# First up projection of a two-block transformer kernel: one 512-column matmul for both parts of the activation

## Chip, cores and metric

The kernel runs on 1 core of one Trainium2 chip. The metric is the device time of one execution in microseconds (us). TensorE, VectorE, ScalarE, GpSimd and SyncE are called PE, DVE, ACT, POOL and SP, as in the profile; PEld is the load of a stationary operand into TensorE.

## What is computed

Two transformer blocks are computed one after the other on 256 tokens of width 2048, in float32. The change lies in the feed-forward part of the first block, and there in the product with `w_up`:

```python
D_FF = 11 * D_MODEL // 4          # 5632

def conv_ffn(h, w_up, w_conv, b_conv, w_down):      # h: (1, 256, 2048)
    z = h @ w_up                                    # (1, 256, 11264)
    z1 = jnp.pad(z[:, :-1], ((0, 0), (1, 0), (0, 0)))
    z2 = jnp.pad(z[:, :-2], ((0, 0), (2, 0), (0, 0)))
    z = w_conv[0] * z2 + w_conv[1] * z1 + w_conv[2] * z + b_conv
    gate, val = jnp.split(z, 2, axis=-1)
    return (jax.nn.gelu(gate) * val) @ w_down

def first_block(x, c, ...):
    ...                                             # modulation vectors, token mixing
    h = rms_norm(x, g_pre_ffn[l]) * (1.0 + sc2) + sh2
    y = conv_ffn(h, w_up[l], w_conv[l], b_conv[l], w_down[l])
    x = x + gt2 * rms_norm(y, g_post_ffn[l])
```

The second block has attention, a state-space scan and a feed-forward part of its own (silu instead of the convolution). It is not changed.

## The kernel before

Each large product is made with two parts of each operand in a rounded format (`float32r`): a high part `hi` and the remainder `lo = x - hi`. A product is then the sum of three matmuls, hi x lo, lo x hi and hi x hi (the helper `three`, lines 2097 to 2101).

**The weights.** All weights stream from HBM as 484 groups of 1 MB, [128, 4, 512] each. SP loads a group into one of four slots (`raw`, line 339) as soon as TensorE has counted the group that used the slot four groups earlier (`pe_used`). ACT makes its high part `w_hi` (line 819), DVE its low part `w_lo` (line 1312), which is written over the raw slot. TensorE waits for `lo_made` at the head of each group (`begin_group`). All engines run an order that is written out by hand; nothing moves on its own.

**The first up projection** (in the profile about 720 to 1225 us) has 22 chunks of 512 weight columns. A chunk is 4 groups; a group is 4 contraction tiles x 4 column tiles x 3 matmuls. Here the weights are the stationary operand and the activation (`h2T_hi`, `h2T_lo`, 256 tokens wide) is the moving one, so each matmul has 256 columns (`cols_chunk`). The result [128, 4, 256] of a chunk fills one of two buffers of two PSUM banks each (`acc0`, `acc1`); the banks `tp0`, `tp1`, `ms0`, `ms1` serve transposes and small things.

**After a chunk** ACT and DVE run `up1(c)`, in this order, with `split()` for the making of a weight part:

| step | ACT | DVE |
|---|---|---|
| 1 | last tap and bias, from PSUM, 4 instructions (L1043) | waits for it (`z_mid`) |
| 2 | `w_hi` of the next chunk's third group | the two other taps, from PSUM, 8 instructions (L1664) |
| 3 | waits for `z_conv`, then gelu (L1050) | `w_lo` of the next chunk's third group |
| 4 | `w_hi` of its fourth group | gate times value (L1672), `w_lo` of the fourth group |
| 5 | high part of the hidden activation (L1054) | its low part (L1678) |
| 6 | `w_hi` of the first two groups of the chunk after that | their `w_lo` |
| 7 | | for the first 16 chunks: `ada_group`, 4 chained instructions on 1 MB of the modulation weights (L1366, L1368) |

So when TensorE ends a chunk, two groups of the next one are ready, and the third becomes ready by steps 1 to 3. The loads of the slots for step 6 are released when TensorE ends the first and the second group of the chunk that it is in. After chunk 21 the down projection starts, in chunks with 512 moving columns; the third group of it is made after `up1(21)`.

**At the entry** (`even_out`) the second chunk holds additional TensorE work whose result nobody reads: 12 matmuls of 512 columns, 8 transposes and the two matmuls of `settle`.

## Time and profile before

| | before |
|---|---|
| median of 3 runs | 3042.03 us (3038.48 to 3045.42) |
| profiled execution: time, span | 3043.16 us, 3041.4 us |
| granted TensorE clock, mean over the span | 0.982 |
| busy: PE, PEld, DVE, ACT, POOL | 96%, 84%, 61%, 42%, 11% |
| chain that ended last: PE, DVE, DMA, ACT | 87%, 6%, 2%, 2% |

A row of the trace gives the start, the length, the engine, the source line, the operation and its operands; brackets at its end hold the time in which the engine was idle before it, and what ended that. Matmuls overlap in the trace: the cost of one in a stream is the distance from its start to the next start, and not its own length. The same holds, to a smaller degree, for instructions on DVE and ACT. The result tile of the up projection, `zc`, has the name `bias_rows` in the profile, since it lies in that buffer.

### The profile page before, as it was taken

Reading aid. Unit: us, or ns where it says so; the run is one execution under the profiler, and the core shown is the slowest. Engines: PE = TensorE matmul, PEld = TensorE weight load, DVE = VectorE, ACT = ScalarE, POOL = GpSimd, SP = SyncE. Lnnn points to the kernel's source line nnn. Section 1 sums busy time; section 2 is a strip of 40 time slices with the busy share of each in tenths; the row PEclk is TensorE's granted clock in tenths of the full one; section 3 lists DMA queues with packets and bytes.
Section 4 is the critical chain, followed back from the end, with each engine's and each line's share of the span. In section 5 each row is a group of like instructions: output and inputs, shape, how many; then the busy total and the mean of one; then the engine's idle time right before and its main releaser. Section 6 shows DMA issues by size and latency. Waiting matters only on the chain.

```text
span 3041.4 us, 42782 instructions
## 1 busy us (share of the span) xinstructions
PE 2932.4 (96%) x17832; PEld 2560.8 (84%) x17832; DVE 1866.7 (61%) x1884; ACT 1268.0 (42%) x1228; POOL 326.9 (11%) x467
## 2 busy tenths in 40 slices
PE   7999999997999999999799999989999999999998
PEld 3687777877999999888687878867889999999886
DVE  5877777796677776554545456755555555555444
ACT  2334544335444444343524333443444434343333
POOL 1000000000000000000104946610000000000000
PEclk9999999998999999999899998989999999999999
DMA  9877877894566655575546652226645555555554
GB/s 408 354 276 277 298 270 293 292 372 175 222 230 239 227 200 183 202 256 207 193 158 215 220 170 77 92 79 221 244 180 184 193 192 194 192 192 207 207 219 166
DMA packets 109903, 667.32 MB, mean 219 GB/s; under 512 B 23504, under 2 KB 25744, under 8 KB 33360
## 3 DMA queue, kind: packets, MB, share of 16 engines
q1 hardware_dynamic: 101584, 626.96, 56.1%
q0 software_dynamic: 8208, 38.80, 3.5%
q8 instruction: 79, 1.29, 0.2%
q14 instruction: 32, 0.26, 0.0%
HBM read 646.24 MB, written 19.48 MB: 219 GB/s over the span
## 4 chain that ended last, share of the span: by engine, by line
PE 87%; DVE 6%; DMA 2%; ACT 2%; SPq 1%; issue 1%; POOL 0%; DVEq 0%; ACTq 0%; POOLq 0%
PE acc L2099 27%; PE acc L2101 27%; PE acc L2100 27%; DVE w_lo L1312 2%; DMA ada<-ada_stream 2%; PE tp L2148 1%; DVE mod_sum L1368 1%; PE ms L2172 1%; ACT w_hi L819 1%; DMA w_raw<-w_stream 1%; PE acc L2645 0%; SPq L440 0%; PE ms L2099 0%; PE ms L2100 0%; PE ms L2101 0%
## 5 line engine op out<-in xcount | busy, mean ns | idle before, releaser
L1312 DVE TENSOR_TENSOR w_lo<-w_raw,w_hi 128x2048 fp32r<-128x2048 f32 (+1 forms) x484 | 1103.9, 2289 | 742.7 <-ACT w_hi L819 723.7
L819 ACT ACTIVATE w_hi<-w_raw 128x2048 fp32r<-128x2048 f32 (+1 forms) x484 | 918.9, 1907 | 895.6 <-DMA w_raw<-w_stream 893.4
L2099 PE MATMUL acc<-h2T_hi,w_lo 128*128 128x256 f32 x2816 | 786.0, 279 | 0.0
L2100 PE MATMUL acc<-h2T_lo,w_hi 128*128 128x256 f32 x2816 | 785.2, 279 | 0.0
L2101 PE MATMUL acc<-h2T_hi,w_hi 128*128 128x256 f32 x2816 | 785.2, 279 | 0.0
L2101 PEld LDWEIGHTS acc<-h2T_hi,w_hi 128*128 128x128 f32 x2816 | 535.4, 190 | 0.0
L2099 PEld LDWEIGHTS acc<-h2T_hi,w_lo 128*128 128x128 f32 x2816 | 529.8, 188 | 0.1
L2100 PEld LDWEIGHTS acc<-h2T_lo,w_hi 128*128 128x128 f32 x2816 | 529.8, 188 | 0.1
L2099 PE MATMUL acc<-w_hi,hid_lo 128*128 128x512 f32 x704 | 274.6, 390 | 0.9 <-DVE w_lo L1312 0.9
L2101 PE MATMUL acc<-w_hi,hid_hi 128*128 128x512 f32 x704 | 274.0, 389 | 0.0
L2100 PE MATMUL acc<-w_lo,hid_hi 128*128 128x512 f32 x704 | 273.9, 389 | 0.0
L2099 PE MATMUL acc<-w_hi,h1T_lo 128*128 128x512 f32 x576 | 232.9, 404 | 10.1 <-DVE w_lo L1312 10.1
L1368 DVE SCALAR_TENSOR_TENSOR mod_sum<-ada,cond,mod_sum 128x512 f32<-128x512 f32 x300 | 225.3, 751 | 24.6 <-DMA ada<-ada_stream 15.5
L2100 PE MATMUL acc<-w_lo,h1T_hi 128*128 128x512 f32 x576 | 226.1, 393 | 0.0
L2101 PE MATMUL acc<-w_hi,h1T_hi 128*128 128x512 f32 x576 | 226.0, 392 | 0.0
L2099 PEld LDWEIGHTS acc<-w_hi,hid_lo 128*128 128x128 f32 x704 | 132.2, 188 | 28.6 <-DVE w_lo L1312 1.3
L2101 PEld LDWEIGHTS acc<-w_hi,hid_hi 128*128 128x128 f32 x704 | 132.2, 188 | 27.7
L2100 PEld LDWEIGHTS acc<-w_lo,hid_hi 128*128 128x128 f32 x704 | 132.2, 188 | 27.1
L2099 PEld LDWEIGHTS acc<-w_hi,h1T_lo 128*128 128x128 f32 x576 | 109.1, 189 | 39.4 <-issue 15.2
L2099 PE MATMUL acc<-w_hi,nT_lo 128*128 128x512 f32 x320 | 126.6, 396 | 5.2 <-DVE w_lo L1312 5.2
L2101 PEld LDWEIGHTS acc<-w_hi,h1T_hi 128*128 128x128 f32 x576 | 109.1, 189 | 23.6
L2100 PEld LDWEIGHTS acc<-w_lo,h1T_hi 128*128 128x128 f32 x576 | 109.3, 190 | 21.8 <-issue 0.5
(530 smaller groups left out, 3869.1 us busy)
## 6 DMA issues: line engine op xcount, KB each, us to landing
w_raw<-w_stream SPq DMA_DIRECT2D x484, 1024.0 KB, 4.8
ada<-ada_stream SPq DMA_DIRECT2D x80, 1024.0 KB, 7.0
ada_first<-ada_stream SPq DMA_DIRECT2D x16, 1024.0 KB, 12.0
g_dram<-gates_out SPq DMA_DIRECT2D x12, 512.0 KB, 7.4
gates_in<-g_dram POOLq DMA_DIRECT2D x12, 512.0 KB, 6.0
bias_rows<-b_in POOLq DMA_DIRECT2D x18, 256.0 KB, 6.7
x_res<-x POOLq DMA_DIRECT2D x2, 2048.0 KB, 12.5
x_dram<-x_res POOLq DMA_DIRECT2D x2, 2048.0 KB, 7.9
```

The lines of the kernel that those rows point to most:

```text
L819: sc.activation(whi[:, s % 4, :, 0:w], raw[:, s % 4, :, 0:w], ACT.Copy).then_inc(hi_made, 1)
L1312: v.tensor_tensor(wlo[:, s % 4, :, 0:w], raw[:, s % 4, :, 0:w], whi[:, s % 4, :, 0:w].bitcast(F32), ALU.subtract).then_inc(lo_made, 1)
L1368: chain(v.scalar_tensor_tensor(macc[:], slots[b][:, q], cond[:, k:k + 1], macc[:], ALU.mult, ALU.add))
L2099: mm(o, sl, mh, start=start, stop=False, skip_group_check=share)
L2100: mm(o, sh, ml, start=False, stop=False, skip_group_check=share)
L2101: return mm(o, sh, mh, start=False, stop=stop, skip_group_check=share)
L2148: ins = tr(t[0:w, c:c + n], src, ident[0:n, 0:n])
L2172: ins = mm(ms[c % 2][:], cond[:, k:k + 1].to_broadcast([P, P]), adaf[n % 4][:, q], start=k == 0, stop=k == KD - 1)
```

## The change

The two matmuls with `w_hi` as the stationary operand become one with 512 moving columns: the high part of the activation and the low part side by side (`h2Tb`). The bank of a column tile then holds two halves of 256 columns whose sum is the result. A chunk takes four whole banks, the four of `acc` and those of `tp` and `ms` in turn (`wide_banks`). DVE adds the halves of each bank into a new SBUF tile `zs` with a reduction and hands it to ACT (`z_sum`); the taps read `zs` instead of PSUM. The banks are given free after this addition. `even_out` and `settle` are gone, a wait is added ahead of the first wide chunk and one ahead of the fourth group of the down projection.

```diff
+        zs = u("z_sum", [P, 4, S], X0 + 8)
...
-        h2T = [u("h2T_hi", [P, KD, S], -B64, F32R), u("h2T_lo", [P, KD, S], 16 - B64, F32R)]
+        h2Tb = u("h2T", [P, 2, KD, S], -B64, F32R)
+        h2T = [h2Tb[:, 0], h2Tb[:, 1]]
...
+        def wide_banks(n):
+            return [t[:] for t in tp + ms] if n % 2 else [acc[i][:, j] for i in range(2) for j in range(2)]
...
 # ScalarE
             def up1(c, last=False):
-                act.wait_ge(pe_used, upc.n * 4 + (G_IN1 + G_MERGE + G_OUT1 + 4))
+                act.wait_ge(sem("z_sum"), upc.n + 1)
...
-                    ins = sc.activation(zc[:, f], bank(upc.slot)[:].rearrange("p a (b s) -> p (a b) s", s=S)[:, f],
+                    ins = sc.activation(zc[:, f], zs[:, f],
...
 # VectorE
             def up1(c, last=False):
-                b = bank(chunks.slot)[:].rearrange("p a (b s) -> p (a b) s", s=S)
+                dve.wait_ge(pe_used, upc.n * 4 + (G_IN1 + G_MERGE + G_OUT1 + 4))
+                for f, b in enumerate(wide_banks(chunks.slot)):
+                    ins = v.reduce_sum(zs[:, f], b.rearrange("p (a s) -> p s a", s=S), AX.X)
+                chain(ins)
+                dve.sem_inc(acc_free, 1)
+                dve.sem_inc(sem("z_sum"), 1)
                 chunks.add()
                 dve.wait_ge(sem("z_mid"), upc.n + 1)
...
-                        ins = v.scalar_tensor_tensor(zc[:, f, sh:S], b[:, f, 0:S - sh], wv, zc[:, f, sh:S],
+                        ins = v.scalar_tensor_tensor(zc[:, f, sh:S], zs[:, f, 0:S - sh], wv, zc[:, f, sh:S],
...
-                dve.sem_inc(acc_free, 1)
                 dve.sem_inc(sem("z_conv"), 1)
...
 # TensorE
-            cols_chunk(h2T, quarters(y1, 0))
-            cols_chunk(h2T, even_out)
-            up_pairs(FC // 2 - 1)
+            def wide_chunk(ahead=None):
+                banks = wide_banks(chunks.slot)
+                chunks.add()
+                for g in range(KD // GK):
+                    if ahead:
+                        ahead(g)
+                    s = begin_group()
+                    for f in range(4):
+                        for q in range(GK):
+                            k = g * GK + q
+                            mm(banks[f][:, 0:S], wlo[:, s, q, f * P:(f + 1) * P], h2T[0][:, k],
+                               start=k == 0, stop=False, skip_group_check=True)
+                            ins = mm(banks[f].rearrange("p (a s) -> p a s", s=S), whi[:, s, q, f * P:(f + 1) * P], h2Tb[:, :, k],
+                                     start=False, stop=k == KD - 1, skip_group_check=True)
+                    end_group(ins)
+
+            pe.wait_ge(acc_free, chunks.n)
+            wide_chunk(quarters(y1, 0))
+            turned()
+            wide_chunk()
+            with engine_loop(pe, FC // 2 - 1, (m, 8), (chunks, 2)) as i:
+                for _ in range(2):
+                    pe.wait_ge(acc_free, chunks.n - 1)
+                    wide_chunk()
...
             def gate2(i):
+                if i == 3:
+                    pe.wait_ge(acc_free, chunks.n - 1)
```

The up projection of the second block keeps the three matmuls of 256 columns.

TensorE, before, the end of the first chunk and the start of the second. The first three rows are one product of a weight tile; the next three are from `even_out`, with `ms` as their output.

```order
L2099 MATMUL acc<-h2T_hi,w_lo 128x256
L2100 MATMUL acc<-h2T_lo,w_hi 128x256
L2101 MATMUL acc<-h2T_hi,w_hi 128x256
L2099 MATMUL ms<-w_hi,w_lo 128x512
L2100 MATMUL ms<-w_lo,w_hi 128x512
L2101 MATMUL ms<-w_hi 128x512
```

TensorE, after, at the same place (`h2T` is now both parts in one tensor; the second chunk writes `tp` and `ms`).

```order
L2457 MATMUL acc<-h2T,w_lo 128x256
L2459 MATMUL acc<-h2T,w_hi 128x512
L2457 MATMUL acc<-h2T,w_lo 128x256
L2459 MATMUL acc<-h2T,w_hi 128x512
L2457 MATMUL tp<-h2T,w_lo 128x256
L2459 MATMUL tp<-h2T,w_hi 128x512
```

Two instructions stand where there were three, the columns are the same 768, and the run at the entry is gone.

DVE, before, from the last `w_lo` of the first chunk's `up1` to the gelu product of the second.

```order
L1312 TENSOR_TENSOR w_lo<-w_raw,w_hi 128x2048 [waits hi_made] x2
L1366 TENSOR_SCALAR mod_sum_0_79<-ada_0_77,cond 128x512 [waits ada_in0]
L1368 SCALAR_TENSOR_TENSOR mod_sum_0_79<-ada_0_77,cond,mod_sum_0_79 128x512 [waits dve_chain] x3
L1664 SCALAR_TENSOR_TENSOR bias_rows<-acc,conv_taps,bias_rows 128x255 [waits dve_chain,z_mid]
L1664 SCALAR_TENSOR_TENSOR bias_rows<-acc,conv_taps,bias_rows 128x255 x3
L1664 SCALAR_TENSOR_TENSOR bias_rows<-acc,conv_taps,bias_rows 128x254 [waits dve_chain]
L1664 SCALAR_TENSOR_TENSOR bias_rows<-acc,conv_taps,bias_rows 128x254 x3
L1312 TENSOR_TENSOR w_lo<-w_raw,w_hi 128x2048 [waits dve_chain,hi_made]
L1672 TENSOR_TENSOR bias_rows<-bias_rows 128x512 [waits z_gelu]
```

DVE, after, the same stretch.

```order
L1317 TENSOR_TENSOR w_lo<-w_raw,w_hi 128x2048 [waits hi_made] x2
L1371 TENSOR_SCALAR mod_sum_0_79<-ada_0_77,cond 128x512 [waits ada_in0]
L1373 SCALAR_TENSOR_TENSOR mod_sum_0_79<-ada_0_77,cond,mod_sum_0_79 128x512 [waits dve_chain] x3
L1664 TENSOR_REDUCE z_sum<-tp 128x256 [waits dve_chain,pe_used]
L1664 TENSOR_REDUCE z_sum<-tp 128x256
L1664 TENSOR_REDUCE z_sum<-ms 128x256 x2
L1674 SCALAR_TENSOR_TENSOR bias_rows<-z_sum,conv_taps,bias_rows 128x255 [waits dve_chain,z_mid]
L1674 SCALAR_TENSOR_TENSOR bias_rows<-z_sum,conv_taps,bias_rows 128x255 x3
L1674 SCALAR_TENSOR_TENSOR bias_rows<-z_sum,conv_taps,bias_rows 128x254 [waits dve_chain]
L1674 SCALAR_TENSOR_TENSOR bias_rows<-z_sum,conv_taps,bias_rows 128x254 x3
L1317 TENSOR_TENSOR w_lo<-w_raw,w_hi 128x2048 [waits dve_chain,hi_made]
L1681 TENSOR_TENSOR bias_rows<-bias_rows 128x512 [waits z_gelu]
```

Four reductions stand between the modulation sums and the taps. The step that released ACT before, the end of TensorE's chunk, now releases DVE, and ACT starts after the reductions.

## Rows read from the trace of the kernel before

**Rows 1.** The page: chain that ended last by line, and a costly group

```profile
PE acc L2099 27%; PE acc L2101 27%; PE acc L2100 27%; DVE w_lo L1312 2%; DMA ada<-ada_stream 2%; PE tp L2148 1%; DVE mod_sum L1368 1%; PE ms L2172 1%; ACT w_hi L819 1%; DMA w_raw<-w_stream 1%; PE acc L2645 0%; SPq L440 0%; PE ms L2099 0%; PE ms L2100 0%; PE ms L2101 0%
...
L2099 PE MATMUL acc<-h2T_hi,w_lo 128*128 128x256 f32 x2816 | 786.0, 279 | 0.0
```

**Rows 2.** Busy time by stretch: us, PE, PEld, DVE, ACT, POOL, clock, DMA, GB/s

```profile
900.00:1000.00 100.00, 100.00 (x851) 100.00 (x850) 72.23 (x78) 44.87 (x42) 0.00 (x0) 1.00 0.62 228
```

**Rows 3.** Timeline of PE in the down projection (start, length)

```profile
1300.06 0.39 PE L2099 MATMUL acc<-w_hi,hid_lo 128*128 128x512 f32 x1
...
1302.78 0.39 PE L2099 MATMUL acc<-w_hi,hid_lo 128*128 128x512 f32 x1
```

**Rows 4.** Timeline of DVE, one chunk of the up projection

```profile
956.36 3.34 DVE L1664 SCALAR_TENSOR_TENSOR bias_rows<-acc,conv_taps,bias_rows 128x255 f32<-128x255 f32 x8 [1.55 <-ACT bias_rows L1043]
959.95 2.29 DVE L1312 TENSOR_TENSOR w_lo<-w_raw,w_hi 128x2048 fp32r<-128x2048 f32 x1 [0.24 <-DVE bias_rows L1664]
962.15 0.68 DVE L1672 TENSOR_TENSOR bias_rows<-bias_rows 128x512 f32<-128x512 f32 x1
962.99 2.29 DVE L1312 TENSOR_TENSOR w_lo<-w_raw,w_hi 128x2048 fp32r<-128x2048 f32 x1
965.20 0.69 DVE L1678 TENSOR_TENSOR hid_lo<-bias_rows,hid_hi 128x512 fp32r<-128x512 f32 x1
966.72 2.29 DVE L1312 TENSOR_TENSOR w_lo<-w_raw,w_hi 128x2048 fp32r<-128x2048 f32 x1 [0.84 <-ACT w_hi L819]
972.37 2.29 DVE L1312 TENSOR_TENSOR w_lo<-w_raw,w_hi 128x2048 fp32r<-128x2048 f32 x1 [3.37 <-ACT w_hi L819]
974.58 3.11 DVE L1368 SCALAR_TENSOR_TENSOR mod_sum<-ada,cond,mod_sum 128x512 f32<-128x512 f32 x4
978.97 3.34 DVE L1664 SCALAR_TENSOR_TENSOR bias_rows<-acc,conv_taps,bias_rows 128x255 f32<-128x255 f32 x8 [1.28 <-ACT bias_rows L1043]
982.56 2.29 DVE L1312 TENSOR_TENSOR w_lo<-w_raw,w_hi 128x2048 fp32r<-128x2048 f32 x1 [0.25 <-DVE bias_rows L1664]
```

**Rows 5.** Timeline of ACT, the same chunk

```profile
954.39 1.93 ACT L1043 ACTIVATE bias_rows<-acc,conv_taps 128x256 f32<-128x256 f32 x4 [4.67 <-PE acc L2101]
...
970.43 1.92 ACT L819 ACTIVATE w_hi<-w_raw 128x2048 fp32r<-128x2048 f32 x1 [3.74 <-DMA w_raw<-w_stream]
977.01 1.93 ACT L1043 ACTIVATE bias_rows<-acc,conv_taps 128x256 f32<-128x256 f32 x4 [4.66 <-PE acc L2101]
```

**Rows 6.** Timeline of SP's DMA queue, issue of the second slot's load

```profile
965.63 0.33 SPq L339 DMA_DIRECT2D w_raw<-w_stream  x1
```

**Rows 7.** Nearest rows for the reductions and for reading SBUF on ACT

```profile
L1445 DVE TENSOR_REDUCE mod_part<-tp 128x4 f32<-128x512 f32 x16 | 11.0, 685 | 4.6 <-PE tp L2148 4.5
...
699.83 0.58 ACT L968 ACTIVATE bias_rows<-acc 128x512 f32<-128x512 f32 x1
...
704.28 0.63 ACT L968 ACTIVATE bias_rows<-x_res 128x512 f32<-128x512 f32 x1 [3.06 <-DVE x_res L1592]
```

**Rows 8.** Timeline of ACT, DVE and PE where the down projection begins

```profile
1225.54 1.94 ACT L1043 ACTIVATE bias_rows<-acc,conv_taps 128x256 f32<-128x256 f32 x4 [4.40 <-PE acc L2101]
...
1234.96 2.29 DVE L1312 TENSOR_TENSOR w_lo<-w_raw,w_hi 128x2048 fp32r<-128x2048 f32 x1 [1.12 <-ACT w_hi L819]
...
1237.31 0.50 PE L2099 MATMUL acc<-w_hi,hid_lo 128*128 128x512 f32 x1 [0.93 <-DVE w_lo L1312]
```

**Rows 9.** Timeline of ACT, starts of the first two `up1`

```profile
746.61 1.93 ACT L1043 ACTIVATE bias_rows<-acc,conv_taps 128x256 f32<-128x256 f32 x4 [5.07 <-PE acc L2101]
...
773.28 1.93 ACT L1043 ACTIVATE bias_rows<-acc,conv_taps 128x256 f32<-128x256 f32 x4 [4.33 <-PE acc L2101]
```

**Rows 10.** Timeline of PE after two waits, and the stretches that follow them

```profile
394.28 0.48 PE L2148 MATMUL tp<-ident,scores 128*128 128x128 f32 x1 [3.44 <-DVE scores L1540]
...
1652.66 0.50 PE L2099 MATMUL acc<-w_hi,nT_lo 128*128 128x512 f32 x1 [2.79 <-DVE w_lo L1312]
...
394.00:400.80 6.80, 6.52 (x15) 4.58 (x16) 5.20 (x9) 4.39 (x6) 0.00 (x0) 0.50 0.40 167
...
1653.50:1657.00 3.50, 3.50 (x10) 2.74 (x9) 1.49 (x1) 3.29 (x3) 3.04 (x7) 0.51 0.56 234
```

More of the change, by code:

```diff
@@ L2406, in _ @@
                     mod_turn(macc2[n - 1])
-            def settle():
-                for t in range(TT):
-                    mm(ms[1][:, t * P:(t + 1) * P], ones[:].to_broadcast([P, P]), ident[:], start=True, stop=True)
             def quarter(src, n):
@@ L2441, in up_pairs @@
                         cols_chunk(h2T)
-            def even_out(g):
-                if g == 0:
-                    s = m.slot % 4
-                    pe.wait_ge(lo_made, m.n + 1)
-                    for q in range(GK):
-                        three(ms[0][:], whi[:, s, q, 0:P], wlo[:, s, q, 0:P], whi[:, s, q], wlo[:, s, q], q == 0, q == GK - 1)
-                if g == 2:
-                    for q in range(8):
-                        tr(ms[1][:, q % 4 * P:(q % 4 + 1) * P], ident[:], ident[:])
-                if g == 3:
-                    settle()
-            cols_chunk(h2T, quarters(y1, 0))
-            cols_chunk(h2T, even_out)
-            up_pairs(FC // 2 - 1)
+            def wide_chunk(ahead=None):
[21 more added lines that the diff above has]
+                    wide_chunk()
             def gate2(i):
+                if i == 3:
+                    pe.wait_ge(acc_free, chunks.n - 1)
                 if 3 <= i <= 6:
```

## The prediction, written before the changed kernel ran

> **What bounds the kernel now.** I read the chain that ended last first. By line, the three matmul lines of the helper `three` hold 27% each of the span [rows 1]; the reader is to see that TensorE sets the time nearly everywhere. The group of the up projections has 0.0 us of idle time before its 2816 instructions [rows 1]. Then I read busy time by stretch inside the first up projection: in 100 us TensorE starts 851 matmuls at a granted clock of 1.00, and DVE is busy for 72 us of them [rows 2]. So TensorE is the bound, but DVE has only 28 us of 100 to spare, and the timelines of DVE, ACT and the DMA queue decide what happens when TensorE gets faster and DVE gets more to do.
>
> The mean length of a matmul (279 ns [rows 1]) is no price. 100 us by 851 starts is 117.5 ns for one with 256 columns [rows 2]. A chunk ends where ACT's first step starts: from 954.39 to 977.01 is 22.62 us [rows 5], by 192 matmuls 117.8 ns. With 512 columns, 12 matmuls lie between 1300.06 and 1302.78 [rows 3]: 226.7 ns.
>
> **Term 1, the matmuls.** Before, a tile costs 3 x 117.8 = 353.4 ns, after 117.8 + 226.7 = 344.5 ns. The columns are the same 768; only one fixed cost of 8.9 ns goes. It doesn't save a third. A chunk has 64 tiles: 0.57 us less, 22.05 us. All 22 chunks: 12.5 us if TensorE never waits.
>
> **Term 2, what DVE and ACT get.** Four reductions of 512 elements each. The nearest row is a reduction that reads 512 elements of PSUM in 685 ns [rows 7], with fewer outputs (4, not 256). Instructions of one kind start a little before the last one's end (a `w_lo` of 2.29 us is followed after 2.21 [rows 4]), so I take 0.61 us each and 2.52 us for four. From the end of a chained instruction over its semaphores to the next is 0.25 us after the taps [rows 4] and 0.16 after the gelu product (962.15 + 0.68 to 962.99 [rows 4]); I take 0.20 from the reductions to ACT. ACT then reads SBUF, not PSUM: 0.63 against 0.58 us for 512 elements [rows 7], 0.2 us for its four. The taps on DVE I leave unchanged.
>
> What hides this? From ACT's first step to the end of the third group's `w_lo` passed 982.56 + 2.29 - 977.01 = 7.84 us [rows 4, 5]. It becomes 2.52 + 0.20 + 7.84 + 0.2 = 10.76, plus 0.06 until TensorE starts (1237.25 to 1237.31 [rows 8]): 10.82. TensorE has two ready groups, 22.05 / 2 = 11.02 us. In a chunk before which DVE is idle it just fits, with 0.2 us to spare, and costs nothing.
>
> In the 16 chunks that follow an `ada_group` DVE isn't idle. It ends the modulation sums at 974.58 + 3.11 = 977.69 [rows 4], 0.68 us after TensorE's chunk. That cost nothing, since ACT came first; now the reductions queue behind it. This makes a closed loop through the ring of slots. TensorE ends the second group and releases its slot's load at 965.63 [rows 6]; ACT's `w_hi` follows at 970.43 [rows 5], then `w_lo`, then the sums to 977.69: 12.06 us. Then 0.16 until the first reduction, 2.52 + 0.20, then 8.04, then 0.06: 23.04 us from the end of a chunk's second group to the start of the next chunk's third. If TensorE waits s there, a chunk takes P = 22.05 + s and the loop spans P + s. So s = (23.04 - 22.05) / 2 = 0.50 us and P = 22.55: against 22.62 only 0.07 us is gained in each. DVE's own work in that period, in series, is 2.52 + 0.20 + 5.75 (ACT's step and the taps) + 2.20 + 0.84 + 2.21 + 0.75 + 2 x 2.21 + 3.11 + 0.16 = 22.16 us [rows 4, 5]. It fits, with 0.4 us to spare, so the load's loop is the tighter one.
>
> The stage: 16 x 0.07 + 6 x 0.57 = 4.5 us gained of the 12.5.
>
> **Term 3, the start of the down projection.** After the last chunk two groups of the down projection are ready. Already TensorE waits 0.93 us for the third [rows 8]. The chain from 1225.54 to the `w_lo` at 1234.96 depends on ACT and DVE alone [rows 8], and it grows by 2.52 + 0.20 + 0.2 = 2.9 us: the wait becomes 3.85, 2.9 us lost, and no work of TensorE's takes its place.
>
> The wait has a second price. A TensorE wait of 3.44 us was followed by a stretch at half clock (1.2 GHz) to 400.8, and one of 2.79 us by 3.5 us at 0.51 [rows 10]. At half clock matmuls take double, so these cost (400.8 - 394.3) / 2 = 3.3 and about 1.7 us. For a wait of 3.85 us I take the middle, 2.5.
>
> **Term 4, the entry run.** The second chunk took 773.28 - 746.61 = 26.67 us [rows 9], 4.05 more than 22.62. This is wholly on TensorE's path, and it goes. The added waits for free banks cost nothing: DVE frees a bank 3 us after a chunk's end, a whole chunk before it is written again, and the transposes' banks are copied before their turn. Two modulation loads start in the same place and come nearer to the next weight loads; up to 1 us, not in the sum.
>
> **The sum**, against the profiled execution's span of 3041.4 us and time of 3043.16: -4.5 + 2.9 + 2.5 - 4.05 = -3.15, giving a time of 3040.0. The median shown is 1.1 us lower, so I forecast 3038.9 us, 0.1% less. I call a difference of under 0.2% (6 us) no difference that this kernel's runs can tell.
>
> **Rivals.**
>
> *The waits don't come, faster.* All 12.5 us arrive if the loop is a microsecond shorter than I make it (by slightly shorter loads or a reduction that costs less), and the clock holds. -12.5 - 4.05 + 2.9 = -13.7: 3028.4 us. For it: the margin is half a microsecond in a loop of 23. Against it: every link of the loop is a row of one chunk, and the reductions can't be much under 512 elements' time. Halfway cases land near 3034.
>
> *The reductions cost by outputs too, slower.* No row shows a reduction with 256 outputs. If each output took a slot beside the inputs, 768 elements: the slope between 512 and 2048 elements, (2.29 - 0.69) / 1536 = 1.04 ns [rows 4], gives 0.95 us each, 3.58 for four, 1.06 more. DVE's series becomes 23.22 and is then the bound of the 16 chunks: +0.60 each, 9.6 us. In the other six the third group comes at 11.88 instead of 11.02, +0.29 each, 1.7. With 2.9 + 1.1 + 2.5 at the down projection and -4.05 this is +13.8: 3055.8 us. It decides against the change from about 0.85 us per reduction. The bounds of the price are these: 0.61 and 0.95; I take the low end, since the row read the same number of elements from the same memory.
>
> *The pair of matmuls costs what three did.* If cost goes with columns (the two parts lie 16 KB apart and no row reads such an operand), 512 columns cost 2 x 117.8 and the chunk stays at 22.62 us. The loop then gives (23.04 + 22.62) / 2 = 22.83 in the 16 chunks, +3.4 us; nothing in the six; +5.4 and -4.05: +4.7, 3046.7 us. For it: the fixed cost of 8.9 ns comes from two stages with different neighbours. Against it: both are long streams at full clock.
>
> The Trainium skill ("TensorE: Matmul & The Clock Gate", Back-to-back issue gap) gives a warm gap of N/2.4 + 2.5 ns. By it the dropped fixed cost is 2.5 ns, 0.16 us a chunk and 3.5 us in all instead of 12.5, which lies between this rival and my Term 1. The rows here show larger gaps, 117.8 against its 109.2 and 226.7 against its 215.8; I go by the rows.
>
> **How the numbers follow.** Forecast 0.50 (3034 to 3044: 0.2 us in the loop is 1.6 us, the clock after the wait 0 to 3.4), faster rival 0.17, slower 0.13, no cheaper pair 0.12, something not seen 0.08. The range 3030 to 3052 leaves out the far ends of the first two rivals. Faster by over 0.2%: 0.17, plus 0.08 from the forecast's lower edge and 0.02 unseen, 0.27. Slower: 0.13 plus 0.02 and 0.04, 0.19. Within: 0.54.
>
> **What the profile after would show.** Starts of TensorE's pairs 344 ns apart. Chunks of about 22.55 us in the first 17 and 22.05 in the last five, with a wait of about 0.5 us on `w_lo` at the third group in 16 of them. Four reductions with a length of 0.69 us, 2.5 together, the first starting when the modulation sums end. A TensorE wait near 3.9 us at the down projection's third group and half clock behind it. The second chunk without its 4 us. I am wrong if the pair is dearer, the reductions take above 0.8 us, or no third group waits.

## The result

| | before | after |
|---|---|---|
| median | 3041.42 us (3025.1 to 3045.42, 12 executions) | 3049.81 us (3047.87 to 3055.81, 12 executions) |
| ratio after / before | | 1.0036, 95% interval 1.0025 to 1.0048 |
| profiled execution: time, span | 3043.16, 3041.4 us | 3050.85, 3049.1 us |
| granted TensorE clock, mean | 0.982 | 0.982 |

The kernel became slower by 8.4 us, 0.28% by the medians and 0.36% by the paired ratio. I had forecast 3038.9 us. The time lies in my range of 3030 to 3052, but a slowdown of over 0.2% was the side to which I gave 0.19.

The page of the changed kernel: the chain that ended last by line, then the two groups of instructions that took over the stage (busy us, mean ns | idle before).

```profile
PE acc L2108 21%; PE acc L2109 21%; PE acc L2110 21%; PE acc L2459 3%; DVE w_lo L1317 3%; DVE mod_sum L1373 2%; DMA w_raw<-w_stream 2%; PE acc L2457 2%; PE ms L2459 2%; PE tp L2459 2%; DMA ada<-ada_stream 2%; PE tp L2157 1%; ACT w_hi L824 1%; PE ms L2181 1%; DVE bias_rows L1674 1%
...
L2459 PE MATMUL acc<-h2T,w_hi 128*128 128x512 f32 x704 | 251.4, 400 | 0.0
...
L2457 PE MATMUL acc<-h2T,w_lo 128*128 128x256 f32 x704 | 199.7, 284 | 1.8 <-DVE w_lo L1317 1.6
```

The three matmul lines have less of the chain than in [rows 1], since L2457 and L2459 took over the stage, and the making of `w_lo`, the modulation sums, the loads and the taps now stand in it. The stage itself, in the columns of [rows 2]:

```profile
900.00:1000.00 100.00, 98.90 (x557) 85.19 (x556) 82.88 (x94) 45.47 (x42) 0.00 (x0) 1.00 0.62 227
```

TensorE is no longer busy all the time, and DVE has 17 us of 100 to spare, not 28. How dear is a pair? Its timeline in an unbroken stretch:

```profile
959.78 0.28 PE L2457 MATMUL acc<-h2T,w_lo 128*128 128x256 f32 x1
959.90 0.40 PE L2459 MATMUL acc<-h2T,w_hi 128*128 128x512 f32 x1
...
960.84 0.28 PE L2457 MATMUL acc<-h2T,w_lo 128*128 128x256 f32 x1
```

Between the two starts of L2457 lie three pairs: 1.06 us / 3 = 353 ns. The three matmuls of before took 3 x 117.8 = 353.4 ns (22.62 us by 192, [rows 5]). The pair costs the same. I had 344.5.

The same chunk boundary as in [rows 4 to 6], after: SP's queue, ACT, DVE, and then TensorE's first matmul of the third group.

```profile
966.83 0.33 SPq L344 DMA_DIRECT2D w_raw<-w_stream  x1
...
989.44 0.33 SPq L344 DMA_DIRECT2D w_raw<-w_stream  x1
...
995.98 0.33 SPq L344 DMA_DIRECT2D w_raw<-w_stream  x1
```

```profile
971.55 1.92 ACT L824 ACTIVATE w_hi<-w_raw 128x2048 fp32r<-128x2048 f32 x1 [2.12 <-DMA w_raw<-w_stream]
981.91 2.08 ACT L1048 ACTIVATE bias_rows<-z_sum,conv_taps 128x256 f32<-128x256 f32 x4 [8.44 <-DVEq L1667]
```

```profile
973.50 2.29 DVE L1317 TENSOR_TENSOR w_lo<-w_raw,w_hi 128x2048 fp32r<-128x2048 f32 x1 [1.47 <-ACT w_hi L824]
975.71 3.11 DVE L1373 SCALAR_TENSOR_TENSOR mod_sum<-ada,cond,mod_sum 128x512 f32<-128x512 f32 x4
978.97 2.48 DVE L1664 TENSOR_REDUCE z_sum<-acc 128x256 f32<-128x512 f32 x4
984.02 3.37 DVE L1674 SCALAR_TENSOR_TENSOR bias_rows<-z_sum,conv_taps,bias_rows 128x255 f32<-128x255 f32 x8 [2.58 <-ACT bias_rows L1048]
987.54 2.29 DVE L1317 TENSOR_TENSOR w_lo<-w_raw,w_hi 128x2048 fp32r<-128x2048 f32 x1
```

```profile
989.89 0.39 PE L2457 MATMUL tp<-h2T,w_lo 128*128 128x256 f32 x1 [0.62 <-DVE w_lo L1317]
...
1245.30 0.79 PE L2108 MATMUL acc<-w_hi,hid_lo 128*128 128x512 f32 x1 [3.65 <-DVE w_lo L1317]
...
1662.47 0.50 PE L2108 MATMUL acc<-w_hi,nT_lo 128*128 128x512 f32 x1 [1.68 <-DVE w_lo L1317]
```

Read it as a chain. The load issued at 966.83 reaches DVE's `w_lo` at 973.50; the modulation sums follow, then the reductions, which start 0.15 us after the sums end. ACT starts at 981.91, and TensorE gets its third group at 989.89 after 0.62 us of idleness. So the closed loop of the forecast is there, with its parts in the order given. The second TensorE row is the boundary to the down projection, where the 0.93 us of [rows 8] became 3.65. Behind it the clock fell:

```profile
1245.30:1251.20 5.90, 5.90 (x14) 4.64 (x15) 5.90 (x3) 3.12 (x2) 0.00 (x0) 0.50 0.11 43
```

**The account** (chunks are counted from 0). From ACT's first step of chunk 0 to that of chunk 21 (21 chunks) it is 1233.46 - 750.45 = 483.0 us. Before it was 1225.54 - 746.61 = 478.9 [rows 8, 9], of which 4.05 were the entry run. So 21 chunks cost 8.1 us more. Chunk 0 itself ends 1.1 us later: TensorE's next matmul starts at 747.51 against 746.41. Of this, 0.56 us was there when chunk 0 started (720.89 against 720.33). The four rows, before and then after:

```profile
720.33 0.56 PE L2099 MATMUL acc<-h2T_hi,w_lo 128*128 128x256 f32 x1
...
746.41 0.39 PE L2099 MATMUL ms<-w_hi,w_lo 128*128 128x512 f32 x1
```

```profile
720.89 0.56 PE L2457 MATMUL acc<-h2T,w_lo 128*128 128x256 f32 x1
...
747.51 0.28 PE L2457 MATMUL tp<-h2T,w_lo 128*128 128x256 f32 x1
```

With -4.05 this is +5.2 us where the down projection starts. The longer wait adds 3.65 - 0.93 = 2.7, the half clock 5.9 / 2 = about 2.95: +10.9. Some 3 us come back at a later place: before, a wait of 2.79 us was followed by 3.5 us at half clock [rows 10]; after, the same wait is 1.68 (the third TensorE row) and no half clock follows, 1.1 + 1.7 us. The sum, +8.0, stands against +7.7 between the spans.

### The profile page after: what moved, and what is told of

Read it like the earlier page. It is cut to its first block, busy times and chain, and to the rows that moved or that the text cites. A ratio compares the mean times of both kernels' runs of the same rounds, so it can differ in the third digit from the quotient of the medians.

```text
span 3049.1 us, 40010 instructions
## 1 busy us (share of the span) xinstructions
PE 2932.6 (96%) x16400; PEld 2492.3 (82%) x16400; DVE 1919.2 (63%) x1972; ACT 1269.5 (42%) x1228; POOL 332.1 (11%) x467
## 4 chain that ended last, share of the span: by engine, by line
PE 81%; DVE 9%; DMA 4%; ACT 3%; issue 1%; SPq 1%; POOL 0%; ACTq 0%; DVEq 0%; POOLq 0%
PE acc L2108 21%; PE acc L2109 21%; PE acc L2110 21%; PE acc L2459 3%; DVE w_lo L1317 3%; DVE mod_sum L1373 2%; DMA w_raw<-w_stream 2%; PE acc L2457 2%; PE ms L2459 2%; PE tp L2459 2%; DMA ada<-ada_stream 2%; PE tp L2157 1%; ACT w_hi L824 1%; PE ms L2181 1%; DVE bias_rows L1674 1%
## 5 line engine op out<-in xcount | busy, mean ns | idle before, releaser
L2108 PE MATMUL acc<-h2T,w_lo 128*128 128x256 f32 x1408 | 389.0, 276 | 0.0
L2109 PE MATMUL acc<-h2T,w_hi 128*128 128x256 f32 x1408 | 388.9, 276 | 0.0
L2110 PE MATMUL acc<-h2T,w_hi 128*128 128x256 f32 x1408 | 388.8, 276 | 0.0
L2110 PEld LDWEIGHTS acc<-h2T,w_hi 128*128 128x128 f32 x1408 | 264.4, 188 | 0.0
L2109 PEld LDWEIGHTS acc<-h2T,w_hi 128*128 128x128 f32 x1408 | 264.3, 188 | 0.0
L2108 PEld LDWEIGHTS acc<-h2T,w_lo 128*128 128x128 f32 x1408 | 264.3, 188 | 0.0
L2459 PE MATMUL acc<-h2T,w_hi 128*128 128x512 f32 x704 | 251.4, 400 | 0.0
L2457 PE MATMUL acc<-h2T,w_lo 128*128 128x256 f32 x704 | 199.7, 284 | 1.8 <-DVE w_lo L1317 1.6
L2459 PEld LDWEIGHTS acc<-h2T,w_hi 128*128 128x128 f32 x704 | 133.5, 190 | 32.6
```

The source lines that it names most:

```text
L2108: mm(o, sl, mh, start=start, stop=False, skip_group_check=share)
L2109: mm(o, sh, ml, start=False, stop=False, skip_group_check=share)
L2110: return mm(o, sh, mh, start=False, stop=stop, skip_group_check=share)
L2457: mm(banks[f][:, 0:S], wlo[:, s, q, f * P:(f + 1) * P], h2T[0][:, k], start=k == 0, stop=False, skip_group_check=True)
L2459: ins = mm(banks[f].rearrange("p (a s) -> p a s", s=S), whi[:, s, q, f * P:(f + 1) * P], h2Tb[:, :, k], start=False, stop=k == KD - 1, ski ...
```

## The experiments

Theory A, formed from the profile after: a pair costs what three did, so TensorE gains nothing, and the additions push the third group's `w_lo` behind TensorE in chunks 2 to 17 and at the down projection. Rival B: the pair would be cheaper if its moving operand, its bank or its neighbour were other than they are. Rival C: the waits come from the new banks and semaphores, and not from the reductions.

### The entry run alone

```diff
-            cols_chunk(h2T, even_out)
+            cols_chunk(h2T)
```

This is the kernel before without `even_out`.

> The kernel before, without even_out and settle alone; three matmuls of 256 columns stay. Theory (the entry run is only its own length): the second chunk takes 22.6 us instead of 26.67, all others stay at 22.61, and the time is 3041.4 - 4.05 = 3037.4. Rival (the entry run also sets the pace of TensorE in the stage, since a matmul of the same shape is seen at 113.3 ns in the second block and at 117.8 here): the pace of all later chunks changes, to 21.76 us a chunk if it becomes 113.3 ns, and the time falls to about 3019; if the pace is now at its worst already nothing changes beyond the 4 us.

Measured: 3019.32 us in the median (3016.78 to 3038.39, 10 executions), ratio 0.9953 [0.9929, 0.9976]. The profiled execution took 3038.39 us, a span of 3036.6, 4.8 less than before's. Six of the ten lie between 3016.8 and 3019.7 and one at 3025.2, far lower than the entry run can explain. The median was no measure of the edit: there were two groups of executions. I ran it again.

> The kernel of e1 again (three matmuls, no entry run), for more executions and another profile. Theory (TensorE takes one of two paces for the stage, 113.3 or 117.8 ns for 256 columns, by the execution): executions in two groups about 19 us apart, near 3018 and 3037, the greater part in the lower group; a profile in the lower group shows chunks of 21.76 us. Rival (the executions near 3018 gain elsewhere): a profile near 3018 shows chunks of 22.61 us.

Measured: 3035.13 us (12 executions: three of 3016.8 to 3017.7, nine of 3034 to 3040.2), ratio 0.9997 [0.9969, 1.0024]. This time the profile fell in the low group. The two profiles of the same kernel, first the higher:

```profile
900.00:1000.00 100.00, 100.00 (x851) 100.00 (x851) 73.45 (x83) 47.00 (x46) 0.00 (x0) 1.00 0.63 231
```

```profile
900.00:1000.00 100.00, 100.00 (x884) 100.00 (x884) 75.23 (x84) 49.36 (x46) 0.00 (x0) 1.00 0.68 250
```

Both show the full granted clock, TensorE busy throughout and no wait, but the second has 884 matmuls in the time in which the first has 851. The counts take in two or three matmuls that are under way at the ends of the stretch, so I price by the chunk, from ACT's first step to the next: 22.61 us by 192 is 117.8 ns for one of 256 columns, 21.76 us is 113.3 ns. Over 22 chunks that is 18.7 us, the distance of the groups. The kernel before has the low group too: of 118 executions of it over all comparisons, 28 lie under 3030 us. So every comparison below is read by its groups, not by its median alone. The first profile, of the upper group as before's is, has a span 4.8 us shorter than before's, near the -4.05 of Term 4.

### The pair alone, without the additions

```diff
-                act.wait_ge(sem("z_sum"), upc.n + 1)
+                act.wait_ge(pe_used, upc.n * 4 + (G_IN1 + G_MERGE + G_OUT1 + 4))
...
-                    ins = sc.activation(zc[:, f], zs[:, f],
+                    ins = sc.activation(zc[:, f], wide_banks(upc.slot)[f][:, 0:S],
...
-                for f, b in enumerate(wide_banks(chunks.slot)):
-                    ins = v.reduce_sum(zs[:, f], b.rearrange("p (a s) -> p s a", s=S), AX.X)
```

The reductions are gone, and ACT and the taps read the first half of each bank. The product with the activation's low part is thus left out of the result; TensorE still makes it.

> The changed kernel without the additions: ACT and DVE read the first half of each bank, so the product of the activation's low part is left out of the result, while TensorE does all of its work as changed. Theory: TensorE's chunks are 22.61 us without stalls, the down projection's third group waits 0.9 us again, only the entry run is gone: 3037.4. Rival (the pair is cheaper, 344.5 ns): 22.05 us a chunk, 12.5 us less, 3025.

```profile
900.00:1000.00 100.00, 100.00 (x568) 86.85 (x567) 72.90 (x81) 47.51 (x46) 0.00 (x0) 1.00 0.63 229
...
1234.14 0.50 PE L2104 MATMUL acc<-w_hi,hid_lo 128*128 128x512 f32 x1 [0.90 <-DVE w_lo L1317]
```

Measured: 3036.13 us (3034.84 to 3040.06), ratio 0.9996 [0.998, 1.0013]. TensorE never waits in the stage. The chunks take 22.61 us, as before, which by 64 is 353.3 ns for a pair. The time is that of the kernel without the entry run in its upper group (3034 to 3040): the pair is worth nothing. The four new banks and TensorE's waits for them are still in this kernel, so it is not they that stall the stage. The wait at the down projection is back at 0.90 us. The difference to the changed kernel, 3049.8 - 3036.1 = 13.7 us, is the price of the additions and their hand-over.

### Three matmuls and the additions

```diff
-                for f, b in enumerate(wide_banks(chunks.slot)):
+                for f in range(4):
+                    b = bank(chunks.slot)[:, f // 2]
...
+            cols_chunk(h2T, quarters(y1, 0))
+            cols_chunk(h2T)
+            up_pairs(FC // 2 - 1)
```

The other half alone: three matmuls of 256 columns in the old two buffers, and the same four reductions. Each adds the halves of a bank, which here are two column tiles, so the result is another one.

> The changed kernel with the three matmuls of 256 columns of before in the place of the pair; the four additions on DVE, their signals and the reads from SBUF stay (each adds the two halves of a bank, which here are two column tiles, so the convolution gets other numbers). Theory (the pair costs what three did, the loss comes from the additions): the same as the changed kernel, 3049.8, with stalls of about 0.9 us at the third group of every second one of 16 chunks. Rival (the pair saves its 0.57 us a chunk and something else ate it): slower than the changed kernel by 5 to 12 us, 3055 to 3062.

Measured: 3046.17 us (3041.76 to 3051.36), ratio 1.0032 [1.0011, 1.0054]. That is 3.6 us under the 3049.8 of the theory. The waits come mostly at the places of after, two more with them, and at the down projection the wait is 3.66 us. This speaks against rival C: with the old banks, and without the added wait ahead of the fourth group, the reductions and their signals still make the waits. It showed something else. Two stretches, and the wait of TensorE that lies between them:

```profile
922.00:942.00 20.00, 20.00 (x179) 20.00 (x178) 16.46 (x21) 8.71 (x9) 0.00 (x0) 1.00 0.66 256
945.00:965.00 20.00, 20.00 (x172) 20.00 (x172) 16.42 (x21) 8.93 (x9) 0.00 (x0) 1.00 0.66 252
...
943.31 0.38 PE L2109 MATMUL acc<-h2T,w_lo 128*128 128x256 f32 x1 [0.65 <-DVE w_lo L1317]
```

With the two or three at the ends taken off, 179 matmuls in 20 us are the pace of 113 ns and 172 that of 118: the pace changed at the wait between them. Chunks with the faster pace in them can be why this kernel lies under the changed one; no run isolates that.

### The modulation sums out of the reductions' way

```diff
                     split()
+                    if between:
+                        between()
                     split()
...
-                up1(c)
-                ada_group(ada3, macc3[c // 4], c % 4)
+                up1(c, between=lambda: ada_group(ada3, macc3[c // 4], c % 4))
```

The changed kernel with the sums between the last two `w_lo` of `up1`, so that `w_lo` is the last of DVE's work ahead of the reductions.

> The changed kernel with the modulation sums of the first 16 chunks made between the last two weight parts instead of behind them. Theory (the loss in the stage is the loop in which the additions queue behind these sums): DVE is idle when TensorE ends a chunk, the stalls at the third group are gone, 16 x 0.49 = 7.8 us less than the changed kernel, 3042. Rival (DVE simply has too much work for a chunk of 22.6 us, whatever its order): the stalls stay and the time is 3048 to 3052.

```profile
989.16 3.11 DVE L1373 SCALAR_TENSOR_TENSOR mod_sum<-ada,cond,mod_sum 128x512 f32<-128x512 f32 x4
992.41 2.29 DVE L1317 TENSOR_TENSOR w_lo<-w_raw,w_hi 128x2048 fp32r<-128x2048 f32 x1
995.13 1.29 DVE L1664 TENSOR_REDUCE z_sum<-tp 128x256 f32<-128x512 f32 x2 [0.42 <-PE ms L2460]
```

Measured: 3040.99 us (3030.32 to 3043.28), ratio 1.0005 [0.9985, 1.0026]. DVE now waits 0.42 us for TensorE, not TensorE for DVE; nearly all chunks take 22.5 to 22.7 us by ACT's steps, and the stage has no waits of TensorE. From ACT's first step of chunk 0 to that of chunk 21 it is 474.7 us against 483.0, 8.3 less (8.1 by the spans, 8.8 by the medians). This is the 8.1 of the account, with the same work left on DVE: the loop through the modulation sums made that loss. Three executions at 3030 to 3033 lie 9 to 12 us under the middle of the others. Their mean granted clock was 0.984 to 0.986, that of the others 0.981 to 0.983. A mean higher by 0.003 is 18 us less at half clock, which by my estimate is worth about 9 us. So they differ by less time at half clock and not by the pace.

### The third group of the down projection made earlier

```diff
-                if not last:
-                    split()
+                split()
...
-                    split()
+                    if n or q:
+                        split()
```

On top of the edit above, on ACT and DVE: the last `up1` makes the third group's parts at step 2 and 3 as every other `up1` does, and the down projection skips that one.

> e4 (changed kernel, modulation sums earlier), and the third group of the down projection made inside the last up1 at the place where the other chunks make theirs. Theory (the 3.6 us wait there and the half clock behind it are the price of the additions on the last chain): the wait is gone or under 0.5 us, no stretch at half clock follows, 5 to 6 us less than e4, 3035. Rival (the wait only moves to the fourth group, since the chain of the last hidden tile is as long): a wait of 2 us or more stays and the gain is under 3 us, 3038 to 3041.

```profile
1230.24 2.29 DVE L1317 TENSOR_TENSOR w_lo<-w_raw,w_hi 128x2048 fp32r<-128x2048 f32 x1
```

Measured: 3035.53 us (3025.45 to 3039.5), ratio 1.0002 [0.9976, 1.0029]. That `w_lo` now starts at 1230.24, and neither a TensorE wait nor half clock is left there. It is 5.5 us less than without the edit by the medians (6.6 by the spans of the profiles). The profile without it had a wait of 3.64 us and 3.4 us at half clock there (3.64 + 1.7 = 5.3).

### Why the pair is not cheaper: four variants without additions

All four start from the kernel of "the pair alone" and leave out the same product. First the two parts side by side in memory, so that the 512 columns are contiguous.

```diff
-        h2Tb = u("h2T", [P, 2, KD, S], -B64, F32R)
+        h2Tb = u("h2T", [P, KD, 2, S], -B64, F32R)
```

> The pair without the additions (product of the activation's low part left out of the result, as in e3), and the two parts of each activation tile side by side in memory, so that the 512 moving columns are one contiguous stretch. Theory (the slow pace of the pair has nothing to do with the operand's two pieces): the same as e3, 3036.1, pairs 353 ns apart. Rival (reading two pieces 16 KB apart makes the column dearer): pairs at 340 ns, 21.8 us a chunk, 18.7 us less, 3017.

Measured: 3037.29 us (3034.19 to 3041.6), ratio 1.0012 [0.9986, 1.0037], and chunks of 22.61 us again. That the operand lay 16 KB apart wasn't the reason. Next the pair cut into two matmuls of 256 columns, each loading the same weights:

```diff
-                            ins = mm(banks[f].rearrange("p (a s) -> p a s", s=S), whi[:, s, q, f * P:(f + 1) * P], h2Tb[:, :, k],
-                                     start=False, stop=k == KD - 1, skip_group_check=True)
+                            for a_ in (1, 0):
+                                ins = mm(banks[f][:, a_ * S:(a_ + 1) * S], whi[:, s, q, f * P:(f + 1) * P], h2Tb[:, a_, k],
+                                         start=False, stop=k == KD - 1, skip_group_check=True)
```

> e3 (four banks per chunk, no additions, low product left out of the result), with the matmul of 512 columns as two of 256 with the same weights, each with a load of its own, into the same halves of the bank. Theory (the pair loses the fast pace by its mix of 256 and 512 columns): executions in two groups again, near 3037 and 3018. Rival (the four banks, or the two halves of a bank, are what takes the fast pace away): all executions near 3036, as e3.

Measured: 3035.69 us (3019.08, 3019.87 and 3023.53, the others 3035 to 3038.9), ratio 0.9994 [0.9966, 1.0022]. The profile, of the upper group, shows 851 matmuls in 100 us, and the low group is back in three of ten. The 20 executions of the two kernels with the pair all lay between 3034.2 and 3041.6, and the split one's upper group at 3035 to 3039: a second load of the same weights costs nothing that can be measured. Then a group's 16 `w_lo` matmuls first, and its 16 of 512 columns after them:

```diff
                                start=k == 0, stop=False, skip_group_check=True)
+                    for f in range(4):
+                        for q in range(GK):
+                            k = g * GK + q
```

> e3 (pair without additions, low product left out of the result) with the 16 matmuls of 256 columns of a group first and then its 16 of 512, instead of one of each in turn. Theory (it is the alternation of the two widths that keeps the pair in the slow pace): long runs of one width take one of the two paces, by the execution, and part of the executions lie near 3018. Rival (a 512-column matmul with the activation moving is always at 235.5 ns): all executions near 3036, with 235.5 in the profile.

The timeline; equal rows are put together, with their count at the end (the end of the window cuts the third). Below it is the stretch:

```profile
899.87 2.03 PE L2458 MATMUL ms<-h2T,w_hi 128*128 128x512 f32 x8
901.74 1.98 PE L2453 MATMUL acc<-h2T,w_lo 128*128 128x256 f32 x16
903.56 0.62 PE L2458 MATMUL acc<-h2T,w_hi 128*128 128x512 f32 x2
...
900.00:1000.00 100.00, 100.00 (x579) 86.99 (x578) 75.76 (x88) 49.29 (x48) 0.00 (x0) 1.00 0.65 242
```

Measured: 3027.34 us (3018.48 to 3029.32, 12 executions), ratio 0.9966 [0.9949, 0.9983]: faster. All twelve lie between the two values of the expectation, 3018 and 3036, so neither side had it right. From the first 512-column row to the first of 256 columns is 1.87 us / 8 = 233 ns; 16 of 256 take 1.82 us, 113.7 ns each. The chunks take 22.19 us, which by 64 is 346.7 ns for a pair's work. What the order changed are mainly the 256-column matmuls: 118 ns in turn with those of 512, 114 in a run of their own; the 512-column ones went from 235 to 233. Last, all matmuls with 512 columns (`w_lo` too times both parts, a third more columns):

```diff
-                            mm(banks[f][:, 0:S], wlo[:, s, q, f * P:(f + 1) * P], h2T[0][:, k],
+                            mm(banks[f].rearrange("p (a s) -> p a s", s=S), wlo[:, s, q, f * P:(f + 1) * P], h2Tb[:, :, k],
                                start=k == 0, stop=False, skip_group_check=True)
-                    for f in range(4):
-                        for q in range(GK):
-                            k = g * GK + q
```

> e3 with both parts of the activation also against the low part of the weights, so that every matmul of the stage has 512 columns (one product more than the kernel needs, the second half of each bank left out of the result). Theory (only mixed widths are tied to the slow pace): two groups of executions, 226.7 ns and 29.0 us a chunk in the lower, 235.5 ns and 30.1 us in the upper: 3036 + 22 x 7.5 = 3202 in the slow pace and 3177 in the fast one. Rival (512 columns of a moving activation are always slow): all near 3202 with 235.5 ns.

```profile
900.00:1000.00 100.00, 100.00 (x430) 80.12 (x429) 54.61 (x64) 36.50 (x37) 0.00 (x0) 1.00 0.48 180
```

Measured: 3198.48 us (3197.24 to 3201.2, 4 executions), ratio 1.0531. The chunks take 29.87 us, by 128 matmuls 233.4 ns for 512 columns in this stage, in a pure stream. No second group showed in four executions. The 226.7 of [rows 3], which I had used, is of another stage, in which the weights are the moving operand. It can't be carried to this one; whether the kind of moving operand is the reason, these runs don't separate.

### The mended pair, and three matmuls in the same order

The full computation of the changed kernel with the grouped order, the sums moved and the third group made earlier (the three edits shown above together).

> The whole changed computation, nothing left out: the pair with each group's 16 matmuls of 256 columns first, the additions, the modulation sums before the last weight part, the down projection's third group made in the last up1. Theory (the three prices found add up): e9's gain over e3, 8.8 us, off e6's 3035.5: 3026.7, some 0.4% under the kernel before, without stalls of TensorE in the stage. Rival (with chunks of 22.2 us DVE's series of 22.2 to 22.5 us becomes the bound): chunks of 22.5 us and stalls in the first 17, 3033.

```profile
900.00:1000.00 100.00, 100.00 (x576) 86.36 (x575) 83.68 (x102) 46.90 (x46) 0.00 (x0) 1.00 0.65 239
```

Measured: 3029.87 us (3018.91 to 3037.85, 12 executions), ratio 0.9977 [0.9957, 0.9997] against before. It is 3.2 us above the expected 3026.7. TensorE is fully busy and the chunks take 22.1 to 22.5 us, though DVE is busy for 84 us of 100. This version has a lower median than both kernels. Beside it the kernel before had its two groups, 8 of 23 executions at 3023 to 3029 and 15 at 3035 to 3045, so the gain is one over the mixture: the mended pair beats the upper group and not the lower. The last kernel asks whether the order, without any pair, does the same: the kernel without the entry run, with a group's 16 matmuls of `w_lo` first, then 16 of `w_hi` by the low part, then 16 by the high part.

> The kernel before without the entry run, and the matmuls of a group ordered by operand (16 with the low weights, 16 and 16 with the high weights) instead of three by three. Theory (grouping takes the 256-column matmuls to 113.3 ns in every execution): 21.8 us a chunk in the profile, all executions near 3018. Rival (the pace of a pure 256-column stream is drawn anew in each execution, whatever the order): two groups near 3018 and 3037 as in e1 and e7.

Measured: 3035.09 us (3018.3, 3019.4 and 3028.4, nine of 3034.5 to 3038), ratio 0.9989 [0.9968, 1.001], chunks of 22.61 us in the profile. The 3028.4 had a mean granted clock of 0.986 and is no execution of the low group. A stream of 256 columns alone keeps its two groups in any order. Against the mended pair its interval overlaps (0.9957 to 0.9997 and 0.9968 to 1.001), so I don't claim that the mended pair beats every form with three matmuls.

## Why the prediction was wrong

**The step that failed is Term 1, the matmuls.** It had a pair at 117.8 + 226.7 = 344.5 ns, and with it a gain of up to 12.5 us. Measured are 353 ns and no gain. The 226.7 was read in the down projection, and it doesn't belong beside the 117.8 of the up projection. The trace of before shows this: in the second block's up projection the same source line, with 256 columns and the same names of its operands, runs at another pace, also at a granted clock of 1.00 (below the two rows, the stretch in the columns of [rows 2]).

```profile
2399.88 0.28 PE L2099 MATMUL acc<-h2T_hi,w_lo 128*128 128x256 f32 x1
...
2401.24 0.28 PE L2099 MATMUL acc<-h2T_hi,w_lo 128*128 128x256 f32 x1
...
2400.00:2500.00 100.00, 100.00 (x885) 100.00 (x884) 55.69 (x38) 41.07 (x28) 0.00 (x0) 1.00 0.54 197
```

Twelve matmuls lie between the two starts, 1.36 us / 12 = 113.3 ns, and 2 x 113.3 is 226.7. So my fixed cost of 8.9 ns has the size of 2 x (117.8 - 113.3) = 9.0: I had taken the price of 512 columns from a stretch that fits the faster pace, and set it against 256 columns in the slower. In the slower pace a 512-column matmul took 235 ns beside one of 256, about twice the 117.8, and the pair costs what three do. In a pure stream of 512 columns here it took 233.4, which is neither 2 x 113.3 nor 2 x 117.8, and that stays open.

I had named the outcome as the rival "the pair of matmuls costs what three did", with a chance of 0.12 and 3046.7 us, which is 3.1 under the measured time. I argued against it that both streams are long and at full clock. They are, and that proved nothing, as the two paces show. My rival's guess that the 16 KB between the parts might cost something was not the reason either, for side by side the columns cost the same. The Trainium skill ("TensorE: Matmul & The Clock Gate", Back-to-back issue gap) has a gap of N/2.4 + 2.5 ns, which it calls that of an isolated matmul; by it the pair would still have saved 2.5 ns. The trace does not agree: a chunk takes 22.61 us with pairs and with threes.

**Term 2, the additions: the mechanism was right, its size too small.** With the measured pair my own loop gives (23.04 + 22.61) / 2 = 22.83 us for a chunk, 3.4 us more in 16. Measured are 8.1. Four parts of the loop can be compared:

| | forecast | measured |
|---|---|---|
| four reductions | 2.52 | 2.48 (each 0.68) |
| from their end to ACT | 0.20 | 981.91 - 981.45 = 0.46 |
| ACT's four from SBUF | +0.2 | 1.93 to 2.08, +0.15 |
| load issue to TensorE's third group | 23.04 | 989.89 - 966.83 = 23.06 |

So nearly every link and their sum came out, and the rival "the reductions cost by outputs too" is refuted: they cost as their inputs do, at the low bound. What I had set to nothing is how the loop closes: I took the release of a slot and the next group's start as one moment. TensorE's rows tell them apart, after (the starts of the second group and of the fourth, with the third between them at 989.89):

```profile
983.45 0.28 PE L2457 MATMUL tp<-h2T,w_lo 128*128 128x256 f32 x1
...
995.65 0.28 PE L2457 MATMUL tp<-h2T,w_lo 128*128 128x256 f32 x1
```

and before, the start of the third group:

```profile
965.29 0.28 PE L2099 MATMUL acc<-h2T_hi,w_lo 128*128 128x256 f32 x1
```

A group takes 22.61 / 4 = 5.65 us. The second ends at 983.45 + 5.65 = 989.10, and its slot's load is issued at 989.44, 0.34 later. The third group's load is issued at 995.98, 0.33 after 995.65, and before it was 0.34 too (965.63 [rows 6] against 965.29), so the lag could have been read ahead of the change. A second, smaller part is the restart: the group that starts after the wait takes 995.65 - 989.89 = 5.76 us and not 5.65, the excess being at its first matmul. The third group was 989.89 - 989.10 = 0.79 us late (0.62 of it idle in the trace, the rest is the modelled end of the last matmul). The two parts, 0.34 and 0.10, lengthen the loop from 23.06 to 23.50 us.

This also gives the pattern, which I had not foreseen. If a third group makes its chunk longer by s, the next chunk is longer by (23.50 - 22.61) - s: the two share 0.89 us. After one large wait (1.0 us, at the third group of chunk 2) they alternate, with a swing that shrinks and grows again, up to chunks of 22.46 and 23.65 us one after the other. The mean is 22.61 + 0.89 / 2 = 23.05, against (1143.22 - 774.63) / 16 = 23.04 measured between ACT's steps. The 23.06 is of the boundary shown; at other late groups the same stretch, from the load's issue to TensorE's start, was 22.70 to 23.45 us, so the close agreement of the means is in part luck. No run isolates the 0.34 us or the 0.10, which are read from these rows; that the loop is the cause was tested by moving the sums, which took away the whole loss in the stage.

**Term 3, the down projection.** The wait was forecast as 3.85 us and is 3.65 (+2.7 against +2.9); the half clock behind it cost 2.95 against 2.5. The mechanism was right and both sizes near; the edit that takes both away gives 5.5 us.

**Term 4, the entry run.** -4.05 was right: without the run the second chunk takes 22.61 us. Not foreseen: chunk 0 ended 1.1 us later, 0.56 of it from work ahead of the stage. Some 0.4 us is pace: before, the fourth group of chunk 0 took 746.41 - 740.97 = 5.44 us, by 48 matmuls 113.3 ns; after, each group took 5.65 us or more.

**The sum** was -4.5 + 2.9 + 2.5 - 4.05 = -3.15. It is +9.2 (chunks 8.1, first chunk 1.1), +2.7, +2.95, -4.05 and some -2.8 at a later wait that became shorter, +8.0. Of the difference of 11.1 us, Terms 1 and 2 together make 12.6: by my own loop the wrong price of the pair makes 7.9 (-4.5 to +3.4) and the rest of the loop 4.7. Term 3 adds 0.3, the later end of the first chunk 1.1. The later wait gives back 2.8, for which I had no term; that is luck and brings the total nearer to the forecast.

## What to carry to other kernels

Before two prices from different stages are subtracted, look whether an instruction that stands in both stages has the same price there: here 256 columns cost 117.8 ns in one and 113.3 in the other, and twice this difference is the whole forecast gain per pair. Fewer instructions for the same columns need not save anything where the loads of stationary operands are hidden already. When an engine gets new work ahead of a hand-over, follow the ring of buffers round once, from the release of a slot to the next release, with the lag of the release and the restart after a wait: here 0.44 us forgotten in a loop of 23 is by the loop's own sum 3.5 of the 8.1 us lost in it. If the loop doesn't fit, moving work that nobody waits for yet (the modulation sums) out of it can give the loss back, here 8.1 us.

## What the runs showed of the hardware

At a full granted clock (1.00) and without any wait TensorE ran one and the same stream of 256-column matmuls with hidden loads at one of two paces: 117.8 ns each (851 in 100 us, the ends counted in) or 113.3 (884). Over this stage it is worth 18.7 us, more than anything the change does. The second block's up projection ran at 113.3 ns in all 14 profiles, whatever the pace of this one. An execution mostly keeps its pace through the stage; in one kernel it changed at waits of 0.6 us (179 and 172 matmuls in 20 us on either side). The low group of times appeared in 28 of 118 executions of the kernel before, in 7 of 10 and 3 of 12 of the same kernel without its entry run, in 2 of 12 with its three matmuls grouped, and in 3 of 10 with the pair split. With alternating widths (changed kernel, the pair without additions in both layouts, the sums moved, the third group earlier) none of 52 executions lay that low. Four of them lay 9 to 12 us under the middle of their kernel's others; these had mean granted clocks of 0.984 to 0.986, against 0.981 to 0.983 of the others. With widths in runs of 16 the 256-column ones went at 114 ns and the 512-column ones at 233. What draws the pace is open: neither the order of the three operands nor the neighbouring bytes settled it, and no run here separates it further.
